# LRU gates as side-by-side pairs of 64-row products, and low-rank gates in three row groups, in a hybrid decoder layer

## What is computed

```python
# RG-LRU: 16 blocks of 64 channels, two gates of each
xc, new_buf = causal_conv(x_in, conv_buf, conv_w, conv_b)
xb = xc.reshape(b_, l_, LRU_BLOCKS, LRU_BLOCK)
r = jax.nn.sigmoid(jnp.einsum('blki,kij->blkj', xb, wa).reshape(b_, l_, LRU_WIDTH) + ba)
i = jax.nn.sigmoid(jnp.einsum('blki,kij->blkj', xb, wx).reshape(b_, l_, LRU_WIDTH) + bx)
log_a = -LRU_C * r * jax.nn.softplus(-lam)
a = jnp.exp(log_a)
u = jnp.sqrt(-jnp.expm1(2.0 * log_a)) * (i * xc)
# h = scan of a * h + u;  y = h * gelu(gate_in)

# GLA: a low-rank gate, rank 16, for 4 heads of 128 key dims
g_log = jax.nn.log_sigmoid(g_low @ gla_w_alpha + gla_b_alpha) / GLA_TAU
```

## Time and profile before

| | |
|---|---|
| median of three runs | 2859.16 us (2858.22 to 2865.95) |
| the profiled execution | 2858.55 us |
| its span, first to last instruction | 2856.4 us |
| mean granted TensorE clock | 0.991 |
| PE busy | 98% |
| PEld busy | 92% |
| DVE busy | 50% |
| POOL busy | 38% |
| ACT busy | 26% |
| DMA | 91 GB/s mean |

### The profile page before, as it was taken

How to read it: one execution, slowest core, us unless ns; L and a number is a source line. 1 busy time by engine, 2 the same in 40 slices (tenths; PEclk the granted TensorE clock), 3 DMA queues, 4 the chain that set the end, 5 groups by cost and what they waited for, 6 DMA issues and landing times.

```text
span 2856.4 us, 43314 instructions
## 1 busy us (share of the span) xinstructions
PE 2790.7 (98%) x18106; PEld 2633.1 (92%) x18106; DVE 1436.6 (50%) x2023; ACT 744.5 (26%) x1423; POOL 1075.4 (38%) x729
## 2 busy tenths in 40 slices
PE   7999999999999999999989999999999999999999
PEld 7999999897979799999867999998989999999998
DVE  7987002333232427722775310425378677677664
ACT  4555001221222201224983221224231000011002
POOL 4332222221211223323551444301248887873221
PEclk9999999999999999999989999999999999999999
DMA  4111222121221352224444433244222222225222
GB/s 127 38 38 39 70 68 60 50 71 52 56 71 36 108 187 78 80 75 127 155 130 143 145 106 98 67 155 126 77 75 62 85 83 61 91 90 184 95 92 78
DMA packets 319568, 259.15 MB, mean 91 GB/s; under 512 B 32906, under 2 KB 290123, under 8 KB 319376
## 3 DMA queue, kind: packets, MB, share of 16 engines
q1 hardware_dynamic: 230976, 153.38, 18.4%
q10 hardware_dynamic: 88400, 103.01, 10.8%
HBM read 198.84 MB, written 57.51 MB: 90 GB/s over the span
## 4 chain that ended last, share of the span: by engine, by line
PE 84%; DVE 7%; ACT 5%; issue 2%; ACTq 1%; DMA 0%; SPq 0%; POOL 0%; DVEq 0%; POOLq 0%
PE PS L971 39%; PE PS L1676 16%; PE PS L1692 8%; PE PS L1005 5%; PE PS L1061 4%; DVE WK L2628 3%; PE PS L1047 2%; PE PS L1069 2%; PE PS L1554 1%; PE PS L1530 1%; PE PS L1084 1%; PE PS L1708 1%; PE PM L1227 1%; PE PS L1247 1%; PE PS L1252 1%
## 5 line engine op out<-in xcount | busy, mean ns | idle before, releaser
L883 POOL CAST Wh<-Wr 128x1024 fp32r<-128x1024 f32 x169 | 193.3, 1144 | 1524.9 <-DMA Wr<-in_w_in 796.5
L971 PE MATMUL PS<-Hh,Wh 128*128 128x384 f32 (+1 forms) x1928 | 635.6, 330 | 7.1 <-POOL Wl L885 2.0
L971 PE MATMUL PS<-Hh,Wl 128*128 128x384 f32 (+1 forms) x1928 | 629.1, 326 | 0.0
L971 PE MATMUL PS<-Hl,Wh 128*128 128x384 f32 (+1 forms) x1928 | 628.7, 326 | 0.0
L885 POOL TENSOR_TENSOR Wl<-Wr,Wh 128x1024 fp32r<-128x1024 f32 x169 | 433.5, 2565 | 13.5
L971 PEld LDWEIGHTS PS<-Hh,Wh 128*128 128x128 f32 x1928 | 362.5, 188 | 11.1 <-issue 5.9
L971 PEld LDWEIGHTS PS<-Hl,Wh 128*128 128x128 f32 x1928 | 362.6, 188 | 0.9 <-issue 0.2
L971 PEld LDWEIGHTS PS<-Hh,Wl 128*128 128x128 f32 x1928 | 362.4, 188 | 0.0
L2628 DVE SCALAR_TENSOR_TENSOR WK<-WK,PS 128x384 f32<-128x384 f32 (+1 forms) x120 | 63.1, 531 | 438.4 <-PE PS L971 269.8
L3238 DVE TENSOR_TENSOR X<-X,PS 128x384 f32<-128x384 f32 (+1 forms) x264 | 136.3, 529 | 128.1 <-PE PS L1692 83.7
L971 PE MATMUL PS<-Yh,Wh 128*128 128x384 f32 (+1 forms) x576 | 187.9, 326 | 1.5 <-DVE Yl L2937 1.5
(11 more groups left out here) (512 smaller groups left out, 5553.4 us busy)
## 6 DMA issues: line engine op xcount, KB each, us to landing
Wr<-in_w_in SPq DMA_DIRECT2D x82, 512.0 KB, 3.8
X<-f_scr SPq DMA_DIRECT2D x11, 1088.0 KB, 5.1
Wr<-in_w_ffn_gate SPq DMA_DIRECT2D x22, 512.0 KB, 3.7
Wr<-in_w_ffn_up SPq DMA_DIRECT2D x22, 512.0 KB, 4.5
Wr<-in_w_ffn_down SPq DMA_DIRECT2D x22, 512.0 KB, 3.7
merged<-WK ACTq DMA_DIRECT2D x16, 544.0 KB, 3.6
WK<-gates ACTq DMA_DIRECT2D x16, 544.0 KB, 5.0
WK<-merged ACTq DMA_DIRECT2D x16, 544.0 KB, 5.8
```

The costliest lines, as they stand in the source:

```text
L883: pool.tensor_copy(Wh[:, n % SLOTS], Wr[:, n % SLOTS]).then_inc(w_hi, 1)
L971: mm = pe.matmul(bank(f"{name}:{g}")[:, 0:n], L[:, w % SLOTS, k, :], R[:, k, t0:t0 + n], start=(k == 0 and i == 0), stop=(last and k == DT ...
```

## The change

The two 64 x 64 blocks of a 128-channel tile are now multiplied apart, as products of 64 rows and 128 columns. For rows 0 to 63 the weights hold gate r's block in columns 0 to 63 and gate i's in 64 to 127; for rows 64 to 127 it is the other way round. So the half h = 0 leaves r on output partitions 0 to 63 and i on 64 to 127, the half h = 1 the reverse, each in a bank of its own. The first token group goes to the two PM banks (with the semaphores l0 and l0_free), the other two to jobs la and lb: four jobs per tile in place of six. ACT reads half banks: six calls for r, six for i, where the input partitions of i are the other half than its output's; the banks are freed by the calls for i. The bias of gate i is loaded with its halves swapped: two DMAs instead of one.

For the low-rank gates the weight tile low holds the 16 columns three times, at rows 0, 32 and 64, and dt at row 96: four loads of 32 columns instead of two of 64. gla_w_alpha is loaded to three row groups (three DMAs per head instead of one), and the token groups 0, 1 and 2 use one row group each. ACT copies rows 0 to 79 of low in the call that copied rows 0 to 15.

```diff
-        banks(f"lr{t}")
-        banks(f"li{t}")
+        for g in (1, 2):
+            jobs.extend([f"la{t}:{g}", f"lb{t}:{g}"])
...
-        NPACK = 17
+        NPACK = 18
...
-        LATE = {"op_hi": ("nrm_hi", DT),
+        LATE = {"wx2": ("l0", 2 * DT),
+                "si_mm": ("l0_free", DT),
+                "op_hi": ("nrm_hi", DT),
...
+                halves = wk(0)[R_BX:R_BX + 1, 0:D].rearrange("r (t two j) -> r t two j", two=2, j=64)
+                for h in range(2):
+                    sp.dma_start(halves[:, :, 1 - h], I["lru_bx"].rearrange("r (t two j) -> r t two j", two=2, j=64)[:, :, h])\
+                        .then_inc(packs, 16)
                 for row, name, n in ((R_CW, "lru_conv_w", CW), (R_CB, "lru_conv_b", 1), (R_BA, "lru_ba", 1),
-                                     (R_BX, "lru_bx", 1), (R_LAM, "lru_lambda", 1), (R_NMIX, "norm_mix", 1),
+                                     (R_LAM, "lru_lambda", 1), (R_NMIX, "norm_mix", 1),
...
                     for h in range(2):
-                        sp.dma_start(YA[64 * h:64 * h + 64, DT:2 * DT, i * P + 64 * h:i * P + 64 * h + 64],
+                        col = 64 * (i if h == 0 else 1 - i)
+                        sp.dma_start(YA[64 * h:64 * h + 64, DT:2 * DT, col:col + 64],
                                       blocks[h]).then_inc(S("wax"), 16)
...
-                    for i, start in enumerate((C_LOW, C_DT)):
-                        tile = I["w_in"][0, :, start:start + 64]
-                        ins = sp.dma_start(Wr[:, n % SLOTS, :, 64 * i:64 * i + 64], tile.rearrange("(k p) m -> p k m", p=P))
-                        ins.then_inc(w_loaded[n % SLOTS] if i else S("dt_in"), 16)
+                    for i, start in enumerate((C_LOW, C_LOW, C_LOW, C_DT)):
+                        tile = I["w_in"][0, :, start:start + 32]
+                        ins = sp.dma_start(Wr[:, n % SLOTS, :, 32 * i:32 * i + 32], tile.rearrange("(k p) m -> p k m", p=P))
+                        ins.then_inc(w_loaded[n % SLOTS] if i == 3 else S("dt_in"), 16)
...
-            def fp32_all(name, lhsT, rhs):
-
+            def head_gates(t):
+
+                if t:
+                    pe.wait_ge(S("l0_free"), t)
                 for g, (t0, n) in enumerate(GROUPS):
-                    free_bank(pe, f"{name}:{g}")
-                    done(pe.matmul(bank(f"{name}:{g}")[:, 0:n], lhsT, rhs[:, t0:t0 + n], start=True, stop=True),
-                         f"{name}:{g}")
+                    for h in range(2):
+                        rows = slice(64 * h, 64 * h + 64)
+                        if g:
+                            name = f"l{'ab'[h]}{t}:{g}"
+                            free_bank(pe, name)
+                        out = bank(name) if g else PM[:, h]
+                        mm = pe.matmul(out[:, 0:n], YA[rows, DT + t, 0:P], XC(t)[rows, t0:t0 + n], start=True, stop=True)
+                        if g:
+                            done(mm, name)
+                        else:
+                            mm.then_inc(S("l0"), 1)
...
-                fp32_all(f"lr{t}", YA[:, DT + t, 0:P], XC(t))
-                fp32_all(f"li{t}", YA[:, DT + t, P:2 * P], XC(t))
+                head_gates(t)
...
-                pe.wait_ge(S(f"wal{h % 2}"), 16 * (h // 2 + 1))
-                fp32_all(f"ga{h}", CB[0:16].rearrange("p k c -> p (k c)")[:, h % 2 * P:h % 2 * P + P], wk(3)[0:16])
+                pe.wait_ge(S(f"wal{h % 2}"), 48 * (h // 2 + 1))
+                for g, (t0, n) in enumerate(GROUPS):
+                    rows = slice(32 * g, 32 * g + 16)
+                    free_bank(pe, f"ga{h}:{g}")
+                    done(pe.matmul(bank(f"ga{h}:{g}")[:, 0:n], CB[rows].rearrange("p k c -> p (k c)")[:, h % 2 * P:h % 2 * P + P],
+                                   wk(3)[rows, t0:t0 + n], start=True, stop=True), f"ga{h}:{g}")
...
-                all_groups(f"lr{t}", wk(2), ACT.Tanh, bias=SC[:, t, 1:2], scale=0.5)
+                for g, (t0, n) in enumerate(GROUPS):
+                    for h in range(2):
+                        rows = slice(64 * h, 64 * h + 64)
+                        if g:
+                            ready(act, f"l{'ab'[h]}{t}:{g}")
+                        else:
+                            act.wait_ge(S("l0"), 2 * t + h + 1)
+                        src = bank(f"l{'ab'[h]}{t}:{g}") if g else PM[:, h]
+                        ins = act.activation(wk(2)[rows, t0:t0 + n], src[rows, 0:n], ACT.Tanh, bias=SC[rows, t, 1:2],
+                                             scale=0.5)
+                link(ins)
...
-                all_groups(f"li{t}", wk(4), ACT.Tanh, bias=SC[:, t, 2:3], scale=0.5)
+                for g in (1, 2, 0):
+                    t0, n = GROUPS[g]
+                    for h in range(2):
+                        rows, other = slice(64 * h, 64 * h + 64), slice(64 - 64 * h, 128 - 64 * h)
+                        src = bank(f"l{'ab'[h]}{t}:{g}") if g else PM[:, h]
+                        ins = act.activation(wk(4)[rows, t0:t0 + n], src[other, 0:n], ACT.Tanh, bias=SC[other, t, 2:3],
+                                             scale=0.5)
+                        if g:
+                            freed(ins, f"l{'ab'[h]}{t}:{g}")
+                ins.then_inc(S("l0_free"), 1)
...
-                act.dma_start(CB[0:16].rearrange("p k c -> p (k c)")[:, h % 2 * P:h % 2 * P + P],
-                              I["gla_w_alpha"][0, :, h * P:(h + 1) * P]).then_inc(S(f"wal{h % 2}"), 16)
+                for i in range(3):
+                    act.dma_start(CB[32 * i:32 * i + 16].rearrange("p k c -> p (k c)")[:, h % 2 * P:h % 2 * P + P],
+                                  I["gla_w_alpha"][0, :, h * P:(h + 1) * P]).then_inc(S(f"wal{h % 2}"), 16)
...
-                for g in range(3):
-                    read(dve, f"li{t}:{g}")
+                dve.wait_ge(S("l0_free"), t + 1)
```

More of the change, by code:

```diff
@@ L872, in split_to @@
                     if WLIST[n][0] == "lowdt":
-                        pool.wait_ge(S("dt_in"), 16)
+                        pool.wait_ge(S("dt_in"), 48)
                     if WLIST[n][0] == "xo" and n < FIRST_W["xo", 0] + SLOTS:
@@ L909, in weight_x @@
                     dst = pairs(wk(5)[0:TS, g * 512:(g + 1) * 512])
-                    pool.tensor_tensor(dst, x, per_head(WJ(c)), ALU.mult).then_inc(S("wx2"), 1)
+                    pool.tensor_tensor(dst, x, per_head(WJ(c)), ALU.mult).then_inc(S_late("wx2"), 1)
                 if part != "state":
@@ L927, in _ @@
             split_to(w0 + DT)
-            pool.wait_ge(S("wx2"), 2)
+            wait_late(pool, "wx2", 2)
             pool.wait_ge(S("x_used"), 2 * TT - 1)
@@ L1298, in _ @@
             b_tok = wk(2).rearrange("p (c n) -> p c n", c=TT + 1)
-            pe.wait_ge(S("dt_in"), 80)
+            pe.wait_ge(S("dt_in"), 112)
             free_bank(pe, "dtt")
@@ L1428, in _ @@
                 if b == 0:
-                    pe.wait_ge(S("wx2"), 2)
+                    wait_late(pe, "wx2", 2)
                 free_bank(pe, name)
@@ L1445, in _ @@
                                    wk(1, 512, b % 2 * 512)[64 * g:64 * g + 64], start=(b == 0), stop=(b == NB - 1))
-                mm.then_inc(S("si_mm"), 1)
+                mm.then_inc(S_late("si_mm"), 1)
                 if b == NB - 1:
@@ L1948, in _ @@
                 ready(act, f"low:{g}")
-                act.activation(wk(3)[0:16, t0:t0 + n], bank(f"low:{g}")[0:16, 0:n], ACT.Copy)
-                freed(act.activation(wk(7)[64:80, t0:t0 + n], bank(f"low:{g}")[64:80, 0:n], ACT.Copy), f"low:{g}")
+                act.activation(wk(3)[0:80, t0:t0 + n], bank(f"low:{g}")[0:80, 0:n], ACT.Copy)
+                freed(act.activation(wk(7)[96:112, t0:t0 + n], bank(f"low:{g}")[96:112, 0:n], ACT.Copy), f"low:{g}")
             for g in range(3):
                 read(act, f"low:{g}")
-            act.dma_start(dt_scr, wk(7)[64:80, 0:T]).then_inc(S("dt_put"), 16)
+            act.dma_start(dt_scr, wk(7)[96:112, 0:T]).then_inc(S("dt_put"), 16)
             for a in range(2):
@@ L2305, in copy_state @@
                 if b >= 2:
-                    act.wait_ge(S("si_mm"), b - 1)
+                    wait_late(act, "si_mm", b - 1)
                     read(act, f"ub{b - 2}")
@@ L2942, in _ @@
             link(dve.memset(DTK, 0.0))
-            dve.wait_ge(S("dt_in"), 80)
+            dve.wait_ge(S("dt_in"), 112)
             ready(dve, "dtt")
@@ L3105, in _ @@
             q = 2 * TT
-            dve.wait_ge(S("si_mm"), NB)
+            wait_late(dve, "si_mm", NB)
             y_state = [mark(dve.tensor_tensor(heads(wk(0, 512, 512 * g)[0:TS]), heads(PM[0:TS, g, :]),
```

## The result

The changed kernel took 2877.56 us (median of 10 executions, 2869.34 to 2884.04) where the kernel before took 2863.28 (10 executions, 2851.86 to 2870.17) on the same chip: ratio 1.0052, 95% interval 1.004 to 1.0064. That is slower by about 14 us; the prediction was 7 us faster. A second measurement of the same two kernels, further down, gave 1.0041 (1.0028 to 1.0053). The profiled execution of the changed kernel took 2881.16 us around a span of 2879.0, against 2858.55 and 2856.4, so the two traces lie 22.6 us apart, 8 more than the medians.

A forecast was written before the change was run, and what follows sets the result against it. PE, busy for 98% of the span, was taken as the bound. LRU stage -7.7, head +0.4, low-rank -1.2, banks +0.6 and +0.6 gave -7.3 us: median 2851.9 us, range 2848.0 to 2857.0.

The forecast's parts named there:

- The products: LRU gate blocks: 64-row products run in pairs 0.01 us apart, a block takes 2.23 us instead of 3.66.
- Rival 3: Gate blocks: 64-row products of different banks don't overlap at 384 columns; 2865.9 us, slower; chance 0.04.
- DVE's own work ... fits in 25.9: LRU tile: DVE's 24.25 us less some 2 us of stall fits the new 25.9-us tile.
- the stall of L2694: DVE in the LRU tile: 2.27 us, held by POOL's split, shrinks when PE runs ahead.
- A 64-row activation has as many columns, so I take the same price: ACT's gate calls: three copies take 1.47 us, six 2.94; both gates add 2.9 us per tile.
- ACT's slack of 2.56 ahead of the Sqrt: LRU tile: ACT's wait for DVE absorbs the longer first gate, all but about 0.5 us.
- The end of the stage: LRU stage: last block 10.0 us earlier, Sqrt +2.1, DVE's last step +0.2; together -7.7 us.
- The head: Kernel start: one more DMA ahead of the x load and shorter runs, +0.4 us, range 0 to 0.6.
- Low-rank: GLA low-rank products: three row groups at once, 1.06 us per head instead of 2.23; only the first counts, -1.2 us.
- waits of L2892: GLA heads 1 to 3: PE's waits for this DVE instruction grow to 1.5 us each, so nothing is gained there.
- The banks: Behind the LRU stage: moved bank turns cost +0.6 us in scores waits and +0.6 at ob2_0's first group.
- Rival 2: LRU tiles: longer 64-row copies make PE wait for la's bank; 2859.7 or 2866.5 us; chance 0.04.

The follow-up runs named there:

- short_splits: Changed kernel with GpSimd's splits of the LRU weight tiles cut to an eighth of their columns (values not the reference's), against the kernel before: ratio 1.0008.
- h_outer: Changed kernel with ACT's gate calls ordered by halves, three groups of one half first; one execution, no ratio; a gate's six calls 2.96 us instead of 3.44.
- the ring: Kernel before with the ring of six banks turned by two places behind the LRU stage: ratio 1.0019, second time 1.001.

## Why the prediction was wrong

**The products: right.** Pairs 0.01 apart, block 2.03 us, low-rank block 0.84. Rival 3 is out.

**"DVE's own work ... fits in 25.9": this step failed.** I took DVE's 24.25 busy us of a 27.35-us tile and subtracted a stall. But the earlier trace rows show that DVE waited for anything outside its own loop only 1.05 us of the tile; its wait of 1.33 for Yh (the next row of the kernel before) is part of the loop, since ACT casts what DVE has just made.

```profile
171.50 2.08 DVE L2798 TENSOR_TENSOR Yl<-YA,Yh 128x1088 fp32r<-128x1088 f32 x1 [1.33 <-ACT Yh L1944]
```

So DVE's loop was 27.35 - 1.05 = 26.3 already, above 25.9. And the stall of L2694 did shrink (2.27 to 0.3), but the splits then met other instructions: held time went from 4.1 to 5.6 us per tile, and 26.3 plus that difference is the 27.7 to 28.0 measured. short_splits shows the reverse: almost no hold, 25.92 us.

**"A 64-row activation has as many columns, so I take the same price": mis-sized.** 0.58 instead of 0.49, twelve calls, 4.0 us more on ACT instead of 2.9. It made the loop through both engines 27.7 us. h_outer gives back 1.0.

**Each engine held against the tile, not the loop through both.** ACT's slack of 2.56 ahead of the Sqrt and its 18 busy us say nothing of a loop in which ACT waits 9 us for y, with the copies of lx and the table load queued behind Yh.

**The end of the stage: -7.7 predicted, +8.6 (290.89 - 280.79, less 1.5 for the head).** The last block came 9.2 us too late for the reasons above. The tail took 32.4 us instead of 25.3, because I measured it from the block; it now hangs on the loop, and ACT reaches the last block 4.4 us later. The rest are the calls (from the first gate call to the Sqrt 12.0 us, 0.8 more than my terms give) and DVE's y, held with the COPY ahead of it by 2.8 more than before, less 0.8 in Yl.

**The head: +0.4 predicted, 1.5 measured** between the first two profiles, of which 1.26 are the two DMAs with 64-element runs (1.51 for 0.25). The seven profiles with the plain load alone spread over 1.45 us.

**Low-rank -1.2, waits of L2892 at 1.6 each: right. The banks: the places were right, the list too short.** Two waits and a vanished one were missing; that they cancel, so that the sum of the waits is the predicted 1.2, is luck. In the time the ring cost some 4 us, the rest unexplained. Rival 2 had PE waiting for the gate calls to free la's bank. PE does wait at the gate products, but for the copies of lx and lg that ACT reads behind Yh (L1932 and L1767, below), so for the loop. No rival named DVE.

The waits of PE in the changed kernel, over the span (us in total, times, longest):

```profile
PE PS L978 <- DVE YA L2931: 4.9, 3, 1.7
PE PS L1098 <- ACT WK L1932: 2.9, 3, 1.3
...
PE PS L1098 <- ACT WK L1767: 2.4, 1, 2.4
...
PE PS L1241 <- ACT WK L2078: 1.3, 2, 0.6
```

**The comparison of two profiles** would have given 22.6 us to the change, where the medians give 14.3 and 13.1.

## What to carry to other kernels

Before time is taken off the bound engine, write down the closed loops of the others (A waits for B waits for A) with their idle time inside the loop counted in, and compare these, not the busy times, with the new period. A stall that another engine's transfer or split causes moves with the phase; assume that it moves, not that it goes. Compare one profile with another only beside a second profile of the same kernel.

## What the chip showed that I had not expected

- Two 64-row ACT calls in different partition halves start 0.58 us apart, in the same half 0.49 (384 columns, out of PSUM).
- Three row groups of 16 rows run at once: six passes end in 0.84 us from start to next, where in sequence they took 2.02.
- A DMA of one row in 64-element runs holds SP's queue for 0.65 to 0.81 us; the same row in one run 0.25.
- A DVE product of 1088 columns takes 1.28 us, and 3.37 with a GpSimd split beside it; a copy of eight columns 0.16 or 0.75.
- At the start of a GLA head TensorE's clock fell to 1.2 GHz for some 3.3 us, behind small products and a wait of 0.3 to 1.7 us, in one run and not in the next of the same kernel.
